# Attention stage: five tiles of staging rows in place of three, packed biases for own-block units; token stage: queries and keys asked for one step sooner

## What is computed

```
proj = rmsnorm(x) @ w_in                      # q,k,v,z,beta,alpha for A; q,k,v for B; gates
A: gated delta rule, both directions, chunks of 64 tokens, 8 heads
B: dilated window attention, three groups of 4 heads (dilation 1, 4, 16):
   scores = (q . k) / 8 - slope[h] * distance     # distance huge where not allowed
   lse = logsumexp(scores); o = softmax(scores) @ v
   the three groups are mixed by softmax over their lse
x += w_out( sig(gA) * W_pA(A) + sig(gB) * W_pB(B) )
x += 16-expert SwiGLU, each expert choosing its tokens;  y = rmsnorm(x)
```

## Time and profile before

| | us |
|---|---|
| median of 3 runs | 2134.45 (2128.19 to 2137.68) |
| profiled execution | 2129.58 |
| span of its records | 2127.9 |
| mean granted TensorE clock | 0.985 |
| token stage, about | 409 to 796 |
| attention stage, about | 796 to 922 |

### The profile page before, as it was taken

How to read it: one execution, slowest core, us unless ns; L and a number is a source line. 1 busy time by engine, 2 the same in 40 slices (tenths; PEclk the granted TensorE clock), 3 DMA queues, 4 the chain that set the end, 5 groups by cost and what they waited for, 6 DMA issues and landing times. The chain is left out here.

```text
span 2127.9 us, 41317 instructions
## 1 busy us (share of the span) xinstructions
PE 2029.4 (95%) x17482; PEld 1651.1 (78%) x17482; DVE 1298.0 (61%) x1512; ACT 884.9 (42%) x1243; POOL 585.1 (27%) x585
## 2 busy tenths in 40 slices
PE   7999999999999997889889999899999999999996
PEld 5778888899999996778746667677777777777774
DVE  6655311125677655745577679766676667666665
ACT  5564211011111115721274442465666556556655
POOL 0000000001588765954554222111111111111200
PEclk9999999999999998899999999999999999999998
DMA  4233322228878768779965433487887888788787
GB/s 152 67 92 102 105 96 102 71 84 228 251 202 237 209 181 249 231 204 290 275 227 183 155 99 129 171 323 283 300 315 286 301 298 327 274 308 309 292 292 278
DMA packets 206409, 456.43 MB, mean 214 GB/s; under 512 B 98804, under 2 KB 133748, under 8 KB 179124
## 3 DMA queue, kind: packets, MB, share of 16 engines
q1 hardware_dynamic: 167316, 385.43, 52.9%
q0 software_dynamic: 14592, 45.70, 7.3%
q10 hardware_dynamic: 24352, 23.21, 4.1%
HBM read 355.94 MB, written 102.24 MB: 215 GB/s over the span
## 5 line engine op out<-in xcount | busy, mean ns | idle before, releaser
L81 DVE TENSOR_TENSOR ex_w_rest<-weights,ex_w_rounded 128x2048 fp32r<-128x2048 f32 x154 | 347.3, 2289 | 118.1 <-ACT ex_w_rounded L3155 118.1
L3155 ACT CAST ex_w_rounded<-weights 128x2048 fp32r<-128x2048 f32 x154 | 287.0, 1907 | 14.5 <-PEq L51 14.5
L3050 PE MATMUL ex_s_acc<-ex_w_rounded,ex_xt 128*128 128x512 f32 x1024 | 288.2, 395 | 0.7 <-DVE ex_xt L81 0.7
L3050 PEld LDWEIGHTS ex_s_acc<-ex_w_rounded,ex_xt 128*128 128x128 f32 x1024 | 188.3, 188 | 50.2 <-issue 13.2
L3050 PE MATMUL ex_s_acc<-ex_w_rest,ex_xt 128*128 128x512 f32 x512 | 158.1, 390 | 0.0
L88 PE MATMUL ch_wide<-normed,ch_w_rounded 128*128 128x512 f32 x384 | 152.9, 398 | 1.3 <-DVE normed_rest L81 1.3
L88 PE MATMUL ch_wide<-normed,ch_w_rest 128*128 128x512 f32 x384 | 152.1, 396 | 0.0
L88 PE MATMUL ch_wide<-normed_rest,ch_w_rounded 128*128 128x512 f32 x384 | 152.0, 396 | 0.0
L3004 POOL DMA_INDIRECT ex_xs<-hn,rt_sample_idx x16 | 21.5, 1341 | 472.4 <-PE ex_s_acc L3095 450.1
L3050 PE MATMUL ex_y_acc<-ex_w_rounded,ex_ht 128*128 128x512 f32 x512 | 147.6, 399 | 1.0 <-DVE ex_ht L81 1.0
L88 PE MATMUL tk_acc<-tk_w_rounded_first,normed 128*128 128x336 f32 x400 | 127.8, 320 | 1.9 <-PEq L51 1.9
(11 more groups left out here) (445 smaller groups left out, 4389.5 us busy)
## 6 DMA issues: line engine op xcount, KB each, us to landing
weights<-in_w_expert SPq DMA_DIRECT2D x154, 1024.0 KB, 8.9
ex_weights<-in_w_expert SPq DMA_DIRECT2D x38, 1024.0 KB, 8.9
laq<-sc_laq ACTq DMA_DIRECT2D x40, 384.0 KB, 4.7
tk_w<-in_w_tok SPq DMA_DIRECT2D x10, 1344.0 KB, 7.2
ch_w<-in_w_ch SPq DMA_DIRECT2D x24, 512.0 KB, 4.4
sc_rows<-rows SPq DMA_DIRECT2D x40, 256.0 KB, 4.3
dl_kv<-qkv_tok SPq DMA_DIRECT2D x40, 256.0 KB, 6.6
dl_qk<-laq SPq DMA_DIRECT2D x20, 512.0 KB, 6.9
```

The costliest lines, as they stand in the source:

```text
L81: return dve.tensor_tensor(out, whole, rounded.bitcast(F32), ALU.subtract)
L3050: mm = pe.matmul(banks[:, b], x[:, k, x_part], w[:, i % SPLIT, kk, 512 * b:512 * b + 512], start=(k == 0 and x_part == 0 and w is w_hi), s ...
L3155: act.copy(w_hi[:, i % SPLIT], raw(i)).then_inc(w_rounded, 1)
```

## The change

The staging rows become a ring of `STAGED` = 5 tiles, so that DVE waits for the store of tile t-5 in place of t-3, with five `stored` semaphores. `LOADED_AHEAD` stays 3 and still paces the loads of values, and `store(t-3)` keeps its place in SP's queue. The room comes from the biases: the three own-block tables move into an array of their own with 128 columns, and everything placed at `EARLY_AT` lies 512 bytes higher. The instructions keep their shapes and counts. In the token stage the q and k of a pair are issued behind the odd step ahead of it instead of with its own even step (the first pair stays with step 0), with the same waits.

```diff
--- before.py
+++ after.py
@@ -619,6 +619,7 @@
 
 
 LOADED_AHEAD = 3
+STAGED = 5
 PAIRS_AHEAD = 2
 UNITS = 3 * NT
 MIXER_AT = (4, 5, 6)
@@ -657,7 +658,7 @@
 
 FIRST_TABLES = [bias_of(ORDER[0], g) for g in range(3)]
 OWN_TABLES = sorted({bias_of(ORDER[u // 3], u % 3) for u in OWN_UNITS})
-EARLY_AT = 195008
+EARLY_AT = 195520
 
 
 def first_column(t):
@@ -686,7 +687,7 @@
 
 def attended_stores(dr, t):
 
-    return sum(16 * len(attended_places(dr, x)) for x in range(t % LOADED_AHEAD, t, LOADED_AHEAD))
+    return sum(16 * len(attended_places(dr, x)) for x in range(t % STAGED, t, STAGED))
 
 
 class FirstPair:
@@ -732,11 +733,12 @@
         v = sb("at_v", [P, V_RING, WINDOWED, GH * HD])
         v_own = sb("at_v_own", [P, OWN_RING, GH * HD])
         distance = spare[:, HELD - 1].rearrange("p k c -> p (k c)").rearrange("p (n c) -> p n c", n=BIASES)
-        bias = sb("at_bias", [P, BIASES, GH, WIN])
+        wide_bias = sb("at_bias", [P, BIASES - len(OWN_TABLES), GH, WIN])
+        own_bias = sb("at_own_bias", [P, len(OWN_TABLES), GH, P])
         s = sb("at_s", [P, 2, GH, WIN])
         p = sb("at_p", [P, 3, GH, WIN])
         pt = spare[:, 3].rearrange("p k c -> p (k c)").rearrange("p (b a h c) -> p b a h c", b=2, a=2, h=GH)
-        stage = sb("at_stage", [P, LOADED_AHEAD, 3, OUT_W])
+        stage = sb("at_stage", [P, STAGED, 3, OUT_W])
         assert next_place(nc) <= EARLY_AT
         q, k, first_distance = first_pair.q, first_pair.k, first_pair.distance
         scores = ps("at_scores", [P, 2, 2, 2, WIN])
@@ -750,6 +752,7 @@
         whole_table = lambda n: first_distance[:, FIRST_TABLES.index(n)] if n in FIRST_TABLES else distance[:, n]
         table_cols = lambda n: slice(PAD, PAD + P) if n in OWN_TABLES else slice(0, WIN)
         table = lambda n: whole_table(n)[:, table_cols(n)]
+        bias = lambda n: own_bias[:, OWN_TABLES.index(n)] if n in OWN_TABLES else wide_bias[:, n, :, table_cols(n)]
         bias_act = [sem(f"at_bias_act{n}") for n in range(BIASES)]
         bias_pool = [sem(f"at_bias_pool{n}") for n in range(BIASES)]
         stored = rows_stored
@@ -807,7 +810,7 @@
                 def store(t):
                     for rows, part in places_of(t):
                         sp.wait_ge(row_done, 3 * t + part[1] + 1)
-                        sp.dma_start(rows, stage[part[0], t % LOADED_AHEAD, part[1], :]).then_inc(stored[t % LOADED_AHEAD], 16)
+                        sp.dma_start(rows, stage[part[0], t % STAGED, part[1], :]).then_inc(stored[t % STAGED], 16)
 
                 sp.wait_ge(tokens_stored, 16 * NT // 2)
                 for t in range(NT):
@@ -842,11 +845,11 @@
                 for n in FIRST_TABLES:
                     pool.wait_ge(distance_loaded[n], 16)
                     for slot in range(2, GH):
-                        pool.tensor_scalar(bias[:, n, slot, table_cols(n)], table(n), slope_of(n, slot), None, ALU.mult).then_inc(bias_pool[n], 1)
+                        pool.tensor_scalar(bias(n)[:, slot], table(n), slope_of(n, slot), None, ALU.mult).then_inc(bias_pool[n], 1)
                 for n in OTHER_TABLES:
                     pool.wait_ge(distance_loaded[n], 16)
                     for slot in range(GH):
-                        pool.tensor_scalar(bias[:, n, slot, table_cols(n)], table(n), slope_of(n, slot), None, ALU.mult).then_inc(bias_pool[n], 1)
+                        pool.tensor_scalar(bias(n)[:, slot], table(n), slope_of(n, slot), None, ALU.mult).then_inc(bias_pool[n], 1)
                 for n in FIRST_TABLES:
                     pool.wait_ge(bias_act[n], 2)
                     pool.wait_ge(bias_pool[n], GH - 2)
@@ -922,7 +925,7 @@
                 def rows_out(u):
                     t, g = u // 3, u % 3
                     act.wait_ge(weighed, u + 1)
-                    act.copy(stage[:, t % LOADED_AHEAD, g, 0:GH * HD], values[:, u % 2, 0:GH * HD]).then_inc(row_done, 1)
+                    act.copy(stage[:, t % STAGED, g, 0:GH * HD], values[:, u % 2, 0:GH * HD]).then_inc(row_done, 1)
 
                 def turned_out(u):
                     if u in OWN_UNITS:
@@ -934,7 +937,7 @@
 
                 def exponentials(u):
                     t, g = u // 3, u % 3
-                    b = t % LOADED_AHEAD
+                    b = t % STAGED
                     act.wait_ge(low_done, u + 1)
                     if u >= 3:
                         act.wait_ge(turned_done, u - 2)
@@ -947,7 +950,7 @@
                 for n in FIRST_TABLES:
                     act.wait_ge(distance_loaded[n], 16)
                     for slot in range(2):
-                        act.activation(bias[:, n, slot, table_cols(n)], table(n), ACT.Copy, scale=slope_of(n, slot)).then_inc(bias_act[n], 1)
+                        act.activation(bias(n)[:, slot], table(n), ACT.Copy, scale=slope_of(n, slot)).then_inc(bias_act[n], 1)
                 for u in range(UNITS + 3):
                     if 0 <= u - 3:
                         rows_out(u - 3)
@@ -970,11 +973,11 @@
                     dve.wait_ge(scored, u + 1)
                     if u >= 2:
                         dve.wait_ge(exp_done, u - 1)
-                    cols, wide = table_cols(n), slice(0, P if u in OWN_UNITS else WIN)
+                    wide = slice(0, P if u in OWN_UNITS else WIN)
                     dve.scalar_tensor_tensor(out=s[:, u % 2, :, wide], in0=scores[:, u % 2].rearrange("p a j c -> p (a j) c")[:, :, wide], scalar=-HD ** -0.5,
-                                             in1=bias[:, n, :, cols], op0=ALU.mult, op1=ALU.add).then_inc(biased, 1)
+                                             in1=bias(n), op0=ALU.mult, op1=ALU.add).then_inc(biased, 1)
                     dve.wait_ge(biased, u + 1)
-                    if g == 0 and t >= LOADED_AHEAD:
+                    if g == 0 and t >= STAGED:
                         dve.wait_ge(stored[b], stores_before(t))
                     low = stage[:, b, g, GH * HD:GH * HD + GH]
                     dve.tensor_reduce(low.rearrange("p (j r) -> p r j", r=2), s[:, u % 2, :, wide].rearrange("p (r j) c -> p r j c", r=2), AX.X, ALU.min).then_inc(low_done, 1)
@@ -1214,11 +1217,11 @@
                         half = side(j, d)
                         sp.dma_start(rows[half, b], dr["rows"][d, chunk:chunk + 1].rearrange("n r t -> (n r) t").partition_broadcast(HD)).then_inc(rows_loaded[b], 16)
                         sp.dma_start(cols[half, b].rearrange("p k h -> p (k h)"), dr["cols"][chunk * CH:chunk * CH + CH, COLS * d:COLS * d + COLS]).then_inc(rows_loaded[b], 16)
-                    if b == 0:
-                        if pair >= 2:
-                            sp.wait_ge(prod_done, pair - 1)
-                        for d, chunk in enumerate(chunks_of(j)):
-                            sp.dma_start(qk[halves[d], pair % 2], dr["qkv_ch"][chunk, :, 0:2 * NH, :]).then_inc(qk_loaded[pair % 2], 16)
+                    for next_pair in [0] if j == 0 else [pair + 1] if b == 1 and j + 1 < STEPS else []:
+                        if next_pair >= 2:
+                            sp.wait_ge(prod_done, next_pair - 1)
+                        for d, chunk in enumerate(chunks_of(2 * next_pair)):
+                            sp.dma_start(qk[halves[d], next_pair % 2], dr["qkv_ch"][chunk, :, 0:2 * NH, :]).then_inc(qk_loaded[next_pair % 2], 16)
 
                 def store_step(j):
                     b = j % 2
@@ -1798,8 +1801,8 @@
                     if p == FIRST_TILE_STEP:
                         for b in range(RING):
                             sp.wait_ge(stored[b], stores_of(b, S_STEPS))
-                        for t in range(NT, NT + LOADED_AHEAD):
-                            sp.wait_ge(rows_stored[t % LOADED_AHEAD], attended_stores(dr, t))
+                        for t in range(NT, NT + STAGED):
+                            sp.wait_ge(rows_stored[t % STAGED], attended_stores(dr, t))
                         first_tile.load(sp, io, dr)
                 for b in range(RING):
                     sp.wait_ge(stored[b], stores_of(b, STEPS))
@@ -3368,7 +3371,7 @@
                 with ExitStack() as delta_ctx:
                     begun = early_loads(nc, delta_ctx, first_pair)
                     late_stored = nc.alloc_semaphore("at_inverse_out")
-                    rows_stored = [nc.alloc_semaphore(f"at_stored{b}") for b in range(LOADED_AHEAD)]
+                    rows_stored = [nc.alloc_semaphore(f"at_stored{b}") for b in range(STAGED)]
                     phase_attention(nc, io, dr, ident, held, begun, load_mixer_first, first_pair, tokens.last_stored, rows_stored, late_stored)
                     phase_delta(nc, io, dr, ident, begun, load_mixer, first_tile, rows_stored, late_stored)
                 phase_merge(nc, io, dr, ident, mixer, mixer_ready, mixer_rest_ready, load_mixer_rest, load_expert, first_tile, routing, held_at)
```

## The result

| | before | after |
|---|---|---|
| median | 2138.01 us (2128.19 to 2147.47, 20 runs) | 2143.18 us (2139.43 to 2151.31, 20 runs) |
| profiled execution | 2129.58 | 2144.39 |
| span of its records | 2127.9 | 2142.7 |

The account below looks back on a forecast made before the run. PE was taken as the bound in the token stage, waits between engines in attention. Stalls 15.3 - new waits 8.4 - clock 1.9 = 5.0 us gained, packed biases and tokens 0, giving 2129.5 us, range 2121 to 2137.

Parts of the forecast that it names:

- The stalls and what follows them: Attention: DVE's staging waits go, up to 15.3 us; new waits take 8.4 and the clock 1.9.
- The new waits: Attention, tiles 4, 6 and 8: PE waits 2.6, 1.7 and 4.0 us for k, taking 8.4 us of the 15.3.
- the rival built on that: Attention: loads move up too, POOL ends the stage with 0.7 us to the barrier; gain at most 9.2 us; 18%.
- the 1.9 of the sum: Attention, behind tile 8's wait: PE's clock falls again, costing 1.9 us, bounds 0 to 2.3.
- the 5.0 of the sum: Whole gain, all in attention: 15.3 (stalls) - 8.4 (new waits) - 1.9 (clock) = 5.0 us.
- It is 4.9 us below the new end and hides behind it.: Attention's end: POOL's issues end at 912.14, 4.9 us below PE's new end at 917.1.
- Everything behind the barrier ... moves with it: After attention: later work is started by its own steps and shifts with the stage's sooner end.
- The slower rival: Attention after tile 8: PE's clock stays low for six units, 13.8 us against 6.9 gained; 6.9 us slower; 4%.
- Tokens, taken at 0: Token stage: issuing q and k sooner changes nothing, at most 0.2 us gained or lost.
- The bounds of 0.2 us: Token stage: at most 0.2 us gained from load waits, at most 0.2 lost if earlier transfers slow a weight load.
- POOL's hides behind PE: Token stage: POOL's one wait of 0.6 us on these loads is covered by PE and gains nothing.
- Unit 17's score: Attention: load_pair(4) needs this score, placed three units ahead of the one at 866.94; argued against POOL ending the stage.

Follow-up runs that it names:

- g2: Kernel before, with the load of the last inverse's blocks issued a tile sooner (tile 2, not 3): ratio 0.9999 to the kernel before.
- g3: Kernel before, with the load of the last inverse's blocks issued a tile later (tile 4): ratio 1.0067 to the kernel before.
- r4: Attention part alone (five staging tiles, packed biases) on the kernel before, token stage unchanged: ratio 1.0010 to the kernel before.
- e5: Attention part alone, with 48 instead of 24 identity products at attention's end: ratio 1.0000 to the kernel before.
- e6: Attention part alone, with the last tile's three stores issued by ACT instead of SP: ratio 1.0023 to the kernel before.
- r1: The kernel before, unchanged, run again: ratio 1.0015 to the kernel before.
- g1: Attention part alone, with the load of the last inverse's blocks issued a tile sooner: ratio 0.9986 to the kernel before.
- e9: Kernel before, with only pair 3's queries and keys in the token stage requested a step sooner: ratio 1.0037 to the kernel before.
- g4: The whole change, with the load of the last inverse's blocks issued a tile sooner: ratio 1.0025 to the kernel before.
- g1b: Second run of g1, the attention part with the last inverse's blocks loaded a tile sooner: ratio 0.9981 to the kernel before.

## Why the prediction was wrong, step by step

- **The stalls and what follows them: right.** DVE's wait for att_out went. The new waits were forecast at tiles 4, 6 and 8 with 2.6, 1.7 and 4.0 us; PE's idle times there are 2.54, 1.78 and 3.54. SP's first q of pair 4 was issued at 69.7 us from the stage's first score, as before (69.2), and took 5.61 us again (5.80), though the scores came sooner. So SP's flow does not hang on PE here, and the rival built on that is out. The Trainium skill's rule on such a record (Perfetto Trace Analysis, section DMA Instruction — HWDGE (DVE, Sync)), that it starts only when the semaphores are satisfied, agrees with these rows. The clock fell behind tile 8 (0.64 from 888.6 to 893.3; that first score took 1.63 in place of 1.13), and tile 8 took 10.7 us to tile 9's first score at 899.38, 1.5 more than undisturbed, against the 1.9 of the sum. PE's part, first score to identity products, fell from 116.5 to 111.3 us, 5.2 against the 5.0 of the sum. Averaged over all executions it is 4.5 where POOL ended the token stage (four each, 116.5 to 111.9) and 3.7 where PE did (six each, 113.4 to 109.7).
- **POOL: "It is 4.9 us below the new end and hides behind it." This step failed, and with it the whole gain.** The term was mis-sized: POOL's chain was taken to end with its issues at 912.14, with 0.7 us to the barrier in the rival. It ends with the landing of its last store, 10.0 us after that was issued at 911.6, and 1.4 us more, as g2 and g3 showed by moving POOL's work alone. With 10.90 us behind the issues in place of 0.7 POOL stood level with PE at 923.1 in the kernel before, and no time of PE in attention was worth anything. The evidence was in the trace of before: POOL's idle time of 10.90 ahead of `dl_state`, one row behind the last one read. I had stopped at the stage's last instruction. The rival's 0.7 us had no row behind it, and its gain was counted from PE's end at 922.06 and not from the delta stage's start at 923.09, which would have given 10.2 and not 9.2.
- **"Everything behind the barrier ... moves with it": failed.** The 5 us saved became idle time at the barrier, 1.03 to 5.89, and PE was granted 0.50 behind it. The first copy into `dl_v` came 4.0 us later. I had weighed the clock only behind waits inside attention. The slower rival had the right mechanism, a low clock of PE, and the wrong place.
- **Tokens, taken at 0: failed in size.** The bounds of 0.2 us looked at who waits for q and k, not at who stands behind them in SP's queue: the next weight block, then the stores and the diagonal blocks' load of another step. "POOL's hides behind PE" overlooked that POOL ends the stage with PE (attention's first score comes 4.0 us behind PE's last product in before, 2.5 or 2.6 where PE is the last). The column of tokens is 1.8 us longer with the whole part (402.5 over five, 400.4 to 404.8, against 400.7 over thirteen, 398.7 to 402.6), so the two overlap; POOL's last scaled keys, above, don't. Attention's column is some 2 us longer where POOL ended the token stage. Two things go with it there: PE starts attention after a longer idle time (3.7 to 7.8 us in place of 2.3) and reaches its second score after 5.5 to 6.9 us in place of 3.9 to 5.6, and POOL's late inverse begins 39.6 to 40.4 us after the first score in place of 36.8 to 38.4 (inverse at its old place). Which of them makes the 2 us was not tried. The time says 1.0013 and 1.0032, a mean of 4.8 us.
- **The sum.** By the times, r4 and its two variants e5 and e6 average 1.0011, 2.3 us, and the tokens part 4.8: 7.1 together, against 6.8 measured for the change. By the columns it is 1.8 + 2 for tokens, 0 for attention and 4 for the cold start: 7.8. That both come near 6.8 is in part luck, since every term is about as large as its own uncertainty. What is shown is that the whole change loses (1.0032 and 1.0030), that the attention stage does not get shorter, and why. How the loss divides between the cold start and the tokens part is argued, not shown. The delta column as a whole is 176.5 (eleven executions with 1.7 us of idle or more) against 167.8 (nine with less), 9 us and not 4. Some 3 of the 9 lie ahead of the first copy and 5 in its steps 10 to 18, which take 6.5 us each undisturbed and up to 11.2. The latter do not come from the clock at the start alone: r1 and g1 had 1.00 there and their first copy after 7.2 us, and still took 172.4 and 176.4. Their cause stays open, as does the size of e9's and g4's loss. What the packed biases do by themselves was not tried.
- **Smaller slips.** Unit 17's score is the one right ahead of the 866.94, at 863.69, not three units ahead; the order that the argument needed holds. A third of 9.3 at 1.98/1.15 costs 2.2 us more, not 2.3. Neither changes the forecast.

## What to carry to other kernels

An engine's part in a stage can end later than its last instruction: here POOL's ended when the last of its stores had landed. Before a wait is taken out of one engine's work, follow every engine across the barrier and compare their idle times there: the one whose idle time is no larger than its own tail sets the end (here 1.03 us for PE, landing plus 0.8 or 0.9 us for POOL), and if it is level with the engine you speed up, move it first. Time saved ahead of a barrier that does not move is idle time for PE, and may be paid for once more in clock. A transfer asked for sooner costs what stands behind it in the queue, not what waits for it.

## What the runs showed of the hardware that was not expected

- At the barrier POOL's idle time follows the slowest landing of its own stores: 7.17 us where that took 6.3 (g3), 10.90 where it took 10.0 (before), 11.65 where it took 10.8 (r1).
- SP's side is different in size: its last store's issue ended 1.5 us ahead of the delta stage in g1, g1b and g4, where POOL and PE had ended sooner. The profile gives no landing for these stores, so whether the barrier waits for it too is not shown.
- PE's granted clock in the first ten microseconds behind the barrier: 1.00 in all nine executions that idled 1.03 to 1.26 us, 0.50 to 0.57 in all five that idled 3.68 to 8.60. Between 1.72 and 2.42 us it was 1.00 twice, 0.66 twice, and 0.51 and 0.52 once each.
- The eight stores of 256 KB took a median of 4.8 us to land where att_out's stores had all been issued before them (g3), and 5.2 to 6.7 beside those in the other twelve; their slowest took 6.3, and 8.0 to 10.8.
